# TensorE's fetch boundary, turn groups of twelve, and an earlier order for the rotated parts and two copies

## The reference

```python
hn   = rmsnorm(h);  p = hn @ W_in        # columns: b_gate, c_gate, x_in (512 each), c_q 384, c_kv 256, k_pe 64
conv = b_gate * dwconv3_causal(c_gate * x_in)
q    = rmsnorm_head(rmsnorm(c_q) @ w_uq)           # 4 heads, 128 plain + 64 rotated columns
k, v = from rmsnorm(c_kv) @ w_ukv and k_pe         # k normed per head; its last 64 columns rotated too
attn = softmax(q k^T * scale, chunk-causal) @ v
h    = h + concat([conv, attn]) @ W_o
h    = h + MoE(rmsnorm(h))                         # top 4 of 32 experts, clamped SwiGLU, d_ff 1024
```

## Time and profile before

| | us |
|---|---|
| median of 3 runs | 2137.09 |
| lowest, highest | 2134.74, 2137.63 |
| the profiled execution, own time | 2136.3 |
| its span in the trace | 2134.5 |
| TensorE busy, of the span | 2066.1 |

### The profile page before, as it was taken

The page is one execution under the profiler, slowest core; times in us unless marked ns, Lnnn a source line. Parts: engine busy times, 40 slices in busy tenths (PEclk is TensorE's granted clock), DMA queues, the critical chain, the costliest instruction groups (busy, mean ns, idle before and its releaser), DMA issues.

```text
span 2134.5 us, 42274 instructions
## 1 busy us (share of the span) xinstructions
PE 2066.1 (97%) x15626; PEld 1892.3 (89%) x15627; DVE 940.4 (44%) x2287; ACT 438.8 (21%) x1083; POOL 572.9 (27%) x650
## 2 busy tenths in 40 slices
PE   7999999999988999999999999999999999999997
PEld 6777778855558999999999999999999999999997
DVE  1233332333454455444444544544554544454544
ACT  1333333232321112111111111111112111112111
POOL 2211111100243233322222333222333222233323
PEclk9999999999989999999999999999999999999999
DMA  7000000051317999999899999989999988999995
GB/s 256 29 11 11 11 11 1 25 188 50 141 59 239 300 313 316 302 288 306 270 297 276 316 284 286 317 281 294 287 318 303 319 284 260 308 318 310 313 302 143
DMA packets 240816, 477.13 MB, mean 224 GB/s; under 512 B 44827, under 2 KB 61223, under 8 KB 240720
## 3 DMA queue, kind: packets, MB, share of 16 engines
q1 hardware_dynamic: 183408, 433.21, 60.8%
q0 software_dynamic: 32784, 39.40, 8.6%
q10 hardware_dynamic: 24576, 3.85, 1.1%
HBM read 450.76 MB, written 30.99 MB: 226 GB/s over the span
## 4 chain that ended last, share of the span: by engine, by line
PE 92%; DVE 3%; issue 2%; ACT 1%; DMA 0%; DVEq 0%; POOLq 0%; POOL 0%; SPq 0%; ACTq 0%
PE psum L1095 42%; PE psum L1111 23%; PE psum L882 8%; PE psum L1029 5%; PE psum L921 4%; PE psum L899 2%; PE psum L963 1%; PE psum L988 1%; PE psum L989 1%; PE psum L1009 1%; PE psum L974 1%; DVE area L1456 1%; DVE area L1451 1%; PE psum L1059 1%; DVE area L1455 1%
## 5 line engine op out<-in xcount | busy, mean ns | idle before, releaser
L1095 PE MATMUL psum<-area 128*128 128x128 f32 (+3 forms) x8192 | 975.5, 281 | 12.8 <-issue 12.5
L1095 PEld LDWEIGHTS psum<-area 128*128 128x128 f32 x8192 | 966.9, 191 | 17.9 <-issue 17.8
L1111 PE MATMUL psum<-area 128*128 128x128 f32 (+3 forms) x4096 | 496.3, 282 | 2.1
L1111 PEld LDWEIGHTS psum<-area 128*128 128x128 f32 x4096 | 484.5, 191 | 11.6 <-DVE area L1456 11.2
L672 POOL DMA_INDIRECT out<-area x160 | 256.9, 1606 | 68.3 <-issue 39.0
L1430 DVE STREAM_TRANSPOSE area<-area 32x320 f32<-32x320 f32 x512 | 257.2, 502 | 15.0
L1437 DVE TENSOR_SCALAR area<-psum,area 128x160 f32<-128x160 f32 x256 | 86.5, 379 | 331.0 <-PE psum L1095 331.0
L1451 DVE TENSOR_SCALAR area<-psum,area 128x160 f32<-128x160 f32 x256 | 86.5, 379 | 266.5 <-PE psum L1095 265.9
L840 ACT ACTIVATE area<-area 128x320 f32<-128x320 f32 x128 | 60.9, 476 | 674.3 <-DVE area L1437 674.3
L658 POOL TENSOR_TENSOR area<-area 128x5 uint32<-128x5 uint32 x32 | 8.2, 255 | 697.6 <-DMA area<-token_lists 697.6
L882 PE MATMUL psum<-area 128*128 128x128 f32 x1536 | 176.7, 276 | 13.6 <-ACT area L759 7.8
(11 more groups left out here) (201 smaller groups left out, 1225.2 us busy)
## 6 DMA issues: line engine op xcount, KB each, us to landing
area<-in_w_gate_up SPq DMA_DIRECT2D x256, 1024.0 KB, 6.9
area<-in_w_down SPq DMA_DIRECT2D x128, 1024.0 KB, 6.7
area<-in_w_in SPq DMA_DIRECT2D x3, 2048.0 KB, 21.1
area<-in_x SPq DMA_DIRECT2D x9, 512.0 KB, 13.6
area<-in_w_o SPq DMA_DIRECT2D x1, 4096.0 KB, 13.0
out<-area SPq DMA_DIRECT2D x8, 512.0 KB, 2.7
normed_rows<-area SPq DMA_DIRECT2D x8, 512.0 KB, 2.6
area<-in_x ACTq DMA_DIRECT2D x7, 512.0 KB, 3.2
```

Source lines behind the costliest of these rows:

```text
L1095: ins = mm(dst, w_gu[piece][:, k, c * P:(c + 1) * P], xT[:, PART * s + k, 0:width], start=(s == 0 and k == 0 and c % 2 == 0), stop=(s == 1 ...
L1111: ins = mm(bank[4 + d // 3][:, (d % 3) * SLOTS:(d % 3) * SLOTS + width], w_dn[q][:, kk, d * P:(d + 1) * P], actT[:, 2 * q + kk, 0:width], ...
```

## The change

The order of steps changes: for blocks from 2 on `QR i-1` comes ahead of `C i`; for block 1 it stays behind `C 1`. ScalarE's copy of the queries moves from `QQ` into `LOW` of the same block, between the squares and the root. VectorE's copy of the keys moves from `QK` to the head of `LOW`. For the last block both stay. On TensorE the alignment moves from the loop's entry to ahead of `RK 7`, and the loop's groups grow from 6 to 12 turns; the other engines keep six.

```diff
+PE_GROUP = 2 * GROUP
+PE_GROUPS = -(-(MAX_TILES + 1) // PE_GROUP)
@@ schedule()
         if i > 1:
-            steps += unit(old + 2) + [("SC", old + 3)]
+            steps += unit(old + 2) + [("SC", old + 3), ("QR", i - 1)]
         steps.append(("C", i))
+        if i == 1:
+            steps.append(("QR", 0))
         if i > 1:
-            steps += [("PV", old + 2), ("TPa", old + 3)]
-        if i:
-            steps.append(("QR", i - 1))
-        if i > 1:
-            steps += unit(old + 3)[1:]
+            steps += [("PV", old + 2), ("TPa", old + 3)] + unit(old + 3)[1:]
@@ ScalarE
+            def queries_out(n):
+
+                act.wait_ge(qq_turned, n + 1)
+                A(qT_n[n % 2], bank[0].rearrange("p (h n) -> p h n", h=HEADS), ACT.Copy).then_inc(qn_ready, 1)
+
@@ ScalarE, kind == "LOW", after the three squares
+                    if n:
+                        queries_out(n - 1)
                     act.wait_ge(c_sq, n * 3 + 3)
                     A(in_sd, in_ms, ACT.Sqrt, bias=eps).then_inc(in_std, 1)
-                if kind == "QQ":
-                    act.wait_ge(qq_turned, n + 1)
-                    A(qT_n[n % 2], bank[0].rearrange("p (h n) -> p h n", h=HEADS), ACT.Copy).then_inc(qn_ready, 1)
+                if kind == "QQ" and n == NT - 1:
+                    queries_out(n)
@@ TensorE
                 if kind == "RK" and n == NT - 1:
+                    pe.addr_align(256, offset=0, max_nops=0)
                     pe.wait_ge(mask_ready, NT)
@@ TensorE, expert loop
             nc.regs_mov(first, 0)
-            pe.addr_align(256, offset=0, max_nops=0)
             nc.br("pe_group", engines=only)
             with nc.body("pe_next_group", valid_engines=only):
-                nc.regs_alu(first, first, GROUP, op=ALU.add)
-                nc.br_lt(first, GROUPS * GROUP, on_true="pe_group", on_false="pe_leave", engines=only)
+                nc.regs_alu(first, first, PE_GROUP, op=ALU.add)
+                nc.br_lt(first, PE_GROUPS * PE_GROUP, on_true="pe_group", on_false="pe_leave", engines=only)
...
-                nc.br_lt(tile, t0 + GROUP, on_true="pe_tile", on_false="pe_end_group", engines=only)
+                nc.br_lt(tile, t0 + PE_GROUP, on_true="pe_tile", on_false="pe_end_group", engines=only)
@@ VectorE
+            def keys_out(n):
+
+                dve.wait_ge(kk_turned, n + 1)
+                V.tensor_copy(kT_n[:, :, n * P:(n + 1) * P], bank[1].rearrange("p (h n) -> p h n", h=HEADS)).then_inc(kn_ready, 1)
@@ VectorE, kind == "LOW", ahead of the wait for the root
+                    else:
+                        keys_out(n - 1)
-                if kind == "QK":
-                    dve.wait_ge(kk_turned, n + 1)
-                    V.tensor_copy(kT_n[:, :, n * P:(n + 1) * P], bank[1].rearrange("p (h n) -> p h n", h=HEADS)).then_inc(kn_ready, 1)
+                if kind == "QK" and n == NT - 1:
+                    keys_out(n)
```

More of the change, by code:

```diff
@@ L1149, in _ @@
             with nc.body("pe_group", valid_engines=only):
-                t0 = nc.snap(first, min_val=0, max_val=(GROUPS - 1) * GROUP)
+                t0 = nc.snap(first, min_val=0, max_val=(PE_GROUPS - 1) * PE_GROUP)
                 nc.regs_mov(tile, t0)
@@ L1155, in _ @@
             with nc.body("pe_no_tile", valid_engines=only):
-                t = nc.snap(tile, min_val=0, max_val=GROUPS * GROUP - 1)
+                t = nc.snap(tile, min_val=0, max_val=PE_GROUPS * PE_GROUP - 1)
                 with pe.If(t < n_tiles + 1):
```

## The result

| us | before | after |
|---|---|---|
| median | 2137.36 (4 runs, 2134.74 to 2138.70) | 2124.01 (4 runs, 2120.91 to 2124.67) |
| profiled execution, its span | 2136.3, 2134.5 | 2120.91, 2119.1 |
| TensorE busy | 2066.1 | 2061.5 |

The ratio is 0.9938, 95% interval 0.9923 to 0.9952: faster by 13.4 us, where 11.4 were forecast (2125.7; measured 2124.0). The profiled execution is the fastest of its four, so the two spans differ by more, 15.4 us. In the changed kernel the lines have moved: C and X are L888, the turns L905, the query copy L718, the key copy L1228, the root L753, the three copies of QR L763 and L765, the reading of TPa L801, the loop's matmuls L1102 and L1118, the tiny table steps of VectorE L1391 to L1410.

What follows compares the result with a forecast made beforehand. TensorE was taken to bound the kernel, 92% of the chain of waits. Terms -3.0 (C side), -5.6 (X side), -0.4 (boundary) and -2.4 (groups) sum to -11.4 us: 2125.7 against 2137.09, range 2121.5 to 2130.5 for 8 in 10.

Steps and rivals of the forecast that it cites:

- Queries ahead of the root: Block stage: the query copy runs ahead of the root's table load, so C waits less; C side 3.0 us saved.
- QR ahead of C: Block stage: C covers ScalarE's three copies of QR, so X stops waiting in blocks 2 to 5; X side 5.6 us saved.
- The term that was mis-sized: Block stage: blocks 2 to 7 together shorten by 8.4 us.
- Boundary: Expert loop's entry: the 318 ns jump over the gap and about 60 ns leave the path, -0.4 us.
- Groups: Expert loop: three of TensorE's five group ends go at 0.79 us each, -2.4 us.
- Nothing behind the moved copies: Block stage: later root, scalings and softmax steps on the other engines cost nothing; bounds 0 and +3 us.
- A (part of the gain comes back): Block stage: later softmax or QR copies reach the path, taking 3 to 6 of 8.6 us; about 2130; chance 0.14.
- B (the fetch holds the entry up): Loop's entry: the code fetch at 644.2 gates it, so the move brings 0.9 us more; 2124.8; chance 0.08, inside the forecast.
- C (the loop no longer fits): Expert loop: TensorE's code outgrows the held blocks and is fetched each turn, +29 us; 2155; chance 0.05.
- D (nothing arrives): Whole kernel: the waits removed turn up elsewhere one for one; 2134 to 2137; chance 0.05.
- Range: Whole kernel: 2121.5 to 2130.5 us for 8 in 10; spread -3.4 to +3.4 for the clock, +3 for leaks.

Runs made afterwards that it cites:

- The copies alone: Only the query and key copies move into LOW, QR stays behind C and the loop is untouched, against the kernel before: 2133.07 us, ratio 0.9976.
- the boundary alone: Only the alignment moves ahead of RK 7, against the kernel before: 2135.86 us, one run; idle before the loop's first matmul, 5.3 us, also holds the wait for tables.
- a neighbour: Changed kernel with the alignment ahead of RK 7 at place 128, not 0, the loop ending in an eighth block: 2142.21 us, ratio 1.0026 to the kernel before.

## Why the prediction was right

- **Queries ahead of the root.** As written: C's waits fell from 4.2 to 0.9 us (block 1), and the 0.2 behind the key copy came. The copies alone made the blocks 3.7 us shorter (4.4 by the medians).
- **QR ahead of C.** As written: 5.1 us of X's waits gone, block 1's 1.3 left, 0.69 in each of blocks 6 and 7 where 0.69 was put. The copies end 2.5 us before C does, as in the text, and 2.7 before X starts. That this needs the keys first was in the text as a wait of 0.2 us; with neither copy moved, the order is a loss of 4.
- **The term that was mis-sized**: 8.4 us for blocks 2 to 7, measured 10.5. I took the idle time for the whole of a wait. The profile counts it from the end of the last matmul, but a matmul that follows directly starts 0.11 us behind its forerunner's start and not 0.27. In block 2 the last of the five turns starts at 126.14 + 4 x 0.11 = 126.58; X would follow at 126.69 and came at 128.12, 1.43 us for an idle time of 1.27. The burst behind a standstill is also 0.10 longer, 7.41 against 7.31 us. That is 0.26 us a wait; eight waits went (three of C, four of X, one of two in each of blocks 6 and 7, less the new one of block 2), 2.1 us. The figure was worked out after the result and from block 2, but the other blocks bear it out: idle times plus 0.26 us for each wait that went give 2.79, 2.03, 1.58, 0.56 and 0.45 us for blocks 3 to 7, and 2.80, 2.04, 1.58, 0.57 and 0.46 were measured.
- **Boundary**: 0.36 for 0.4. The 5.01 us before the first matmul became 4.72, not 4.6, for the reason given with the boundary alone. The fetch gave nothing, and the jump is hidden behind the wait for the mask (3.49 us, 3.36 before).
- **Groups**: 2.4 in the text, 2.5 of idle time and 2.6 by the loop's length. The three idle times decide for the recorded durations. By the branch figures of the Trainium skill ("Advanced Engine Details and Errata", section Control Flow Timing) it would have been an estimated 1.2.
- **Nothing behind the moved copies** turned up: no new wait of CT, S or BC. In block 7 ScalarE stands 0.54 us for the query turns, 0.4 in the text.
- **Rivals.** A (part of the gain comes back): nothing did. B (the fetch holds the entry up): refuted. C (the loop no longer fits): true of a neighbour, with another price. D (nothing arrives): refuted.
- **Range.** The clock was put as the only large spread. A second one of the same size was overlooked, VectorE against GpSimd in front of the loop (3.0 against 3.1 us between the two profiles of the changed kernel). The kernel before shows it as well, L1397 at 1.52 us. That the median fell within 2 us of the forecast owes something to the runs: the same kernel gave 2124.0 the first time and 2127.3 the second, both inside the range.

## What to carry to other kernels

When two engines hand PSUM back and forth, look at what stands ahead of the short copy on its engine: a table load or a scaling that nobody awaits can keep the bottleneck waiting. Here the reordering on TensorE paid only with the matching one on the other engines. Price a removed wait of TensorE by the distance of starts, not by its idle time, and expect that a long wait which you add may cost the clock as well. Count the instructions of a resident loop before you shift it.

## What the runs showed of the hardware

- **A wait can cost the clock on top.** In the blocks, standstills of 3.4 and 2.7 us were followed by 3.4 us at 1.2 GHz, which cost 1.6 us each; 1.9 and 1.2 us were not. No length of a single wait parts the cases: in the kernel before, the lower level also starts at 523.4 us, behind a wait of 1.69 us, and the wait of 2.35 us near 431 us in the changed kernel has 3.4 us at the lower level behind it in one profile (441.0 us) and none in the other.
- **Held code.** A loop of 1,637 instructions over seven blocks is fetched once: 33 fetches in the whole changed kernel, none after 1010 us. With its end in an eighth block, 16 more blocks are fetched, and two turns have 6.8 and 6.9 us of standstill in front of them. The loop that outgrew the store did not pay at each turn but in four clusters of fetches.
- **GpSimd can hold a VectorE step up until it is done.** A VectorE step of 0.36 us took 4.06 while GpSimd copied 128x1024 and cleared 128x1280. Not every step is held: L1408 runs at its usual 0.27 us inside the same copy that holds L1409. The Trainium skill, "SBUF — State Buffer", section "SBUF: two separate sides", calls the shared port pair an exclusive lock, so that the loser waits for the whole instruction; by that rule the trace agrees on the end, the step ended 0.1 us after the clearing. On the start it leaves a question open: the step began 0.7 us before the copy's recorded start and had time for its 0.36 us, so what held it until the copy began is not shown.
